# Pairing the two directions of a recurrence window by window, and loading the next phase's first strips early

## The reference

```
def _rwkv7_step(state, inp):
    r, w, k, v, kk, a = inp
    sa = jnp.einsum("dbhvk,dbhk->dbhv", state, kk)
    state = (state * w[..., None, :] - sa[..., None] * (kk * a)[..., None, :]
             + v[..., None] * k[..., None, :])
    return state, jnp.einsum("dbhvk,dbhk->dbhv", state, r)
```

## Time and profile before

| | |
|---|---|
| median of 3 runs | 6579.88 us (6574.34 to 6580.43) |
| the profiled execution | 6581.77 us, span 6579.9 us |
| PE busy | 5670.6 us, 86% of the span |
| DVE, ACT, POOL busy | 2987.5, 2063.0, 1877.6 us |
| mean granted TensorE clock | 0.935 of full speed |
| a tile of the recurrence (x2 of window 0 to the next tile's) | 1089.66 to 1242.65 us |
| the two recurrences | about 740 to 2053 us, and 5151 to 6463 us of the span |

### The profile page before, as it was taken

The page is one execution under the profiler, slowest core; times in us unless marked ns, Lnnn a source line. Parts: engine busy times, 40 slices in busy tenths (PEclk is TensorE's granted clock), DMA queues, the critical chain, the costliest instruction groups (busy, mean ns, idle before and its releaser), DMA issues. The chain is left out here.

```text
span 6579.9 us, 214205 instructions
## 1 busy us (share of the span) xinstructions
PE 5670.6 (86%) x92720; PEld 3807.5 (58%) x92720; DVE 2987.5 (45%) x6387; ACT 2063.0 (31%) x3451; POOL 1877.6 (29%) x2006
## 2 busy tenths in 40 slices
PE   5999788888887899977888895698999888888887
PEld 4555577777774455444554454544454677777773
DVE  7100366666663233145534367522300466666661
ACT  3000255454541312133422132311100354544440
POOL 4452144444441336000002631000000344444440
PEclk8999899999998999988899997899999899999998
DMA  3222100001112222122212237522112001110002
GB/s 130 100 90 84 45 31 31 31 31 43 36 37 76 106 100 79 44 84 68 60 48 91 95 96 96 127 72 85 65 65 74 35 31 39 37 39 31 31 31 93
DMA packets 192660, 425.81 MB, mean 65 GB/s; under 512 B 24384, under 2 KB 108224, under 8 KB 192192
## 3 DMA queue, kind: packets, MB, share of 16 engines
q1 hardware_dynamic: 157440, 322.85, 16.5%
q10 hardware_dynamic: 34752, 96.51, 3.7%
HBM read 313.41 MB, written 105.87 MB: 64 GB/s over the span
## 5 line engine op out<-in xcount | busy, mean ns | idle before, releaser
L382 PE MATMUL ps<-arena 128*128 128x512 f32 x4544 | 1686.0, 533 | 60.4 <-ACT arena L336 18.4
L382 PEld LDWEIGHTS ps<-arena 128*128 128x128 f32 x4544 | 862.9, 190 | 878.7 <-issue 810.5
L1890 PE MATMUL ps<-arena 64*64 64x64 f32 x35840 | 737.1, 226 | 172.1 <-issue 75.9
L158 POOL TENSOR_TENSOR arena<-arena 128x512 f32<-128x512 f32 (+1 forms) x360 | 338.9, 957 | 1700.3 <-DMA arena<-w_mod 1690.1
L1890 PEld LDWEIGHTS ps<-arena 64*64 64x64 f32 x35840 | 644.3, 138 | 244.7 <-issue 229.9
L2297 ACT COPY arena<-ps 128x512 f32<-128x512 f32 (+1 forms) x880 | 535.8, 626 | 411.7 <-PE ps L1890 403.1
L2442 POOL TENSOR_TENSOR arena<-arena 128x256 f32<-128x256 f32 (+1 forms) x320 | 316.6, 997 | 812.5 <-DVE arena L2683 533.7
L540 PE MATMUL ps<-arena 128*128 128x512 f32 (+1 forms) x1152 | 422.9, 527 | 18.2 <-ACT arena L336 18.2
L2367 POOL MEMSET arena<- 128x1280 f32 (+4 forms) x22 | 15.1, 739 | 1331.2 <-POOLq L88 1331.2
L161 POOL TENSOR_TENSOR arena<-arena 128x256 f32<-128x256 f32 (+2 forms) x504 | 376.5, 759 | 51.2 <-issue 0.2
L1698 ACT COPY arena<-ps 128x1280 f32<-128x1280 f32 (+1 forms) x64 | 75.0, 1172 | 963.5 <-PE ps L382 749.0
(11 more groups left out here) (269 smaller groups left out, 9762.3 us busy)
## 6 DMA issues: line engine op xcount, KB each, us to landing
arena<-proj SPq DMA_DIRECT2D x158, 640.0 KB, 5.1
proj<-arena ACTq DMA_DIRECT2D x80, 640.0 KB, 3.8
arena<-w_mod SPq DMA_DIRECT2D x96, 512.0 KB, 7.4
arena<-rw_w SPq DMA_DIRECT2D x68, 512.0 KB, 3.4
xres<-arena ACTq DMA_DIRECT2D x24, 640.0 KB, 6.1
arena<-na_w_in SPq DMA_DIRECT2D x24, 512.0 KB, 3.6
arena<-x SPq DMA_DIRECT2D x16, 640.0 KB, 6.7
arena<-xres SPq DMA_DIRECT2D x16, 640.0 KB, 6.0
```

The lines of the kernel that those rows point to most:

```text
L158: self.nc.gpsimd.tensor_tensor(out, strip[:, c:c + n, :], self.k.cond[:, c:c + n, s:s + 1].to_broadcast([P, n, P]), ALU.mult)
L382: last = nc.tensor.matmul(k.ps[:, 3 * u + n, 0:b - a], w[:, c * P:(c + 1) * P], src[:, c, a:b], start=(c == 0), stop=(c == KT - 1))
L1890: last = PE.matmul(part_of(out, dst, hh, g, d), part(l, src, hh, g, d), rhs, start=True, stop=True)
```

## The change

Window n now treats forward chunk group n together with backward group BACK[n] = (0, 4, 3, 2, 1)[n], so that the states of both directions can be carried inside the windows: each trip of PE's loop carries the four steps of the window before it. The separate 20 steps disappear. Maps of one window are kept in place of five. With it:

- BH against KK and BH against R are one set of 16 matmuls of 128 columns (the joined score set), in place of two sets of 64 columns.
- v differs between directions, so v has four transposes in place of two, and `local_outputs` 48 matmuls in place of 40.
- ACT takes over DVE's negated half behind `gh_mm` and the negated copy `zt`; DVE gets the steps and `state_outputs`; POOL gets `second_outputs` (where two directions meet in y) and, inside windows 0 to 3, `gate_values`, `keep_par`, `bonus_half` and `bonus_terms`.
- What is left between windows is the next tile's preparation and one normalisation. It now stands ahead of a tile's windows, also for the first tile; after the last tile the last four steps and two normalisations follow, one after the other.
- SP loads the output projection's first two strips and residual tiles (`early_loads`) once the last tile's operands are used; `dense_residual` waits for `k.early` in their place.

```diff
-STEPS_BACK = [c for s in ((0, NCTX // C), (NCTX // C, NCH)) for c in reversed(range(*s))]
-LOOP_FILL = (0, 24)
+BACK = (0, 4, 3, 2, 1)
+LOOP_FILL = (70, 69)
...
+            def step(n):
+                for d in range(2):
+                    at, col = map_of(d, n) * C, chunk_of(d, n) * C
+                    for hp in HP:
+                        PE.matmul(state_reads(d)[hp, col:col + C], Sst[hp, n % 2, d, :], QT[hp, at:at + C], start=True, stop=True)
+                    for hp in HP:
+                        last = PE.matmul(state_sums(d)[hp, :], TT[hp, at:at + C], Sst[hp, n % 2, d, :], start=True, stop=True)
+                    last.then_inc(s_mm[d], 1)
...
                 product(low[0], Yb, F, 2).then_inc(f2_mm, 1)
-                scores(low[1], BH_, R_).then_inc(m4_mm, 1)
+                pe.wait_ge(yw_ev, it + 1)
+                pe.wait_ge(q_ev, it + 1)
+                step(0)
                 pe.wait_ge(f2_ev, it + 1)
                 product(low[0], F, None, 3).then_inc(di_mm, 1)
+                states_seen(it, 1)
+                step(1)
...
+                states_seen(it, 3)
+                step(3)
                 pe.wait_ge(yzt_ready, it + 1)
                 pe.wait_ge(kb_ev, it + 1)
                 product(low[2], Ya, F, 5).then_inc(f3_mm, 1)
+                pe.wait_ge(y_ev, it + 2)
+                pe.wait_ge(v_kept, it + 1)
+                for d in range(2):
+                    for g in range(2):
+                        PE.transpose(bank[7][...], v_win[:, d, g * P:(g + 1) * P], k.ident)
+                        last = PE.transpose(bank[6][...], ops[:, KK_, d, g * P:(g + 1) * P], k.ident)
+                last.then_inc(kv_mm, 1)
...
+                    step(late, it, 0)
+                    step(late, it, 1)
+                    if n == 0:
+                        weighted(e)
+                    if n == 1:
+                        finished(e)
                     if n + 2 < NW2:
                         sums_scan(e, n + 2)
+                    step(late, it, 2)
                     if more:
                         operands_beta(e, n + 1)
+                    if n:
+                        step(late, it, 3)
+                    else:
+                        restart(it)
+                    state_outputs(late)
...
+                    for half in range(2):
+                        last = SC.mul(flat(RH[:, 4 * half:4 * half + 4, :]), bank[4 + half], -1.0)
+                    last.then_inc(gh_ev, 1)
...
+            for dst_, src_ in early:
+                sp.dma_start(dst_, src_).then_inc(k.early, 16)
```

More of the change, by code:

```diff
@@ L429, in _ @@
                 u = c % 2
+                if c < 2 and early:
+                    continue
                 if c >= 2:
@@ L1826, in tile_loads, with post_loads @@
                 sp.dma_start(par, dram_tile(k.A["rw_par"], e + (KT * j + off))).then_inc(tile_in, 16)
[L1828 to L1832, removed]
+            def post_loads(e, off):
+                sp.wait_ge(bonus_mm, e * 3 + 3)
+                for n, dst_ in ((0, r2), (1, k2)):
+                    sp.dma_start(dst_, dram_tile(k.proj, e + (n * KT + off))).then_inc(post_rk_in, 16)
@@ L1914, in gains @@
                                          RH[cp, hh * 4 + q, C:2 * C], start=False, stop=True)
[L1915 to L1919, removed]
+                last.then_inc(tt_mm, 1)
             def local_outputs():
[L1922 to L1928 removed]
@@ L1938, in turned_scores, with window @@
             def turned_scores():
-                scores(low[1], BH_, KK_).then_inc(xt_mm, 1)
-            def window(it, late, scored):
+                for d in range(2):
+                    for g in range(2):
+                        for hh in range(2):
+                            for c in range(2):
+                                at, col = (2 * g + c) * C, (g * 2 + d) * C
+                                last = PE.matmul(halves(pair[1][HP[c], hh, :])[:, :, col:col + C], ops[HP[hh], BH_, d, at:at + C],
+                                                 ops[HP[hh], KK_:R_ + 1, d, at:at + C], start=True, stop=True)
+                last.then_inc(xt_mm, 1)
+            def window(it, scored):
                 pe.wait_ge(xt_ev, it + 1)
@@ L2373, in betas @@
-            def betas(e, n, first=False):
+            def betas(e, n):
                 if n == 0:
@@ L2424, in keep_par, with second_outputs @@
                 pool.drain()
-            widen_kk(0)
-            betas(0, 0, True)
-            keys(0, 0)
-            keep_v(0, 0, True)
+            def second_outputs(unit, it):
+                pool.wait_ge(y_ev, it + 1)
+                hold(k, pool)
+                for d in range(2):
+                    if not first_touch(d, unit):
+                        at = y[:, cols((unit, BACK[unit])[d])]
+                        GP_.tensor_tensor(at, at, yt[:, d, :], ALU.add)
+                pool.drain().then_inc(y_sum, 1)
             for e in range(KT):
@@ new lines, in _ @@
+                sums_scan(e, 0)
+                sums_rest(e, 0)
+                for c in range(3):
+                    centred(e, MEAN_BANK, c)
+                for c in range(3):
+                    kk_unit(e, c)
+                bonus(e, BONUS_BANK, 0)
+                operands_beta(e, 0)
+                operands_kk(e, 0)
+                variance(e, VAR_BANK)
+                operands_r(e, 0)
+                bonus(e, BONUS_BANK, 1)
+                bonus(e, BONUS_BANK, 2)
+                post_inverse(e)
@@ L2793, in _ @@
-                mask_rest()
-                operands_keys(e + 1, 0)
-                sums(e + 1, 1)
+            it = KT * NW2 + 1
+            carried(NW2 - 1, it)
+            for c in range(3):
+                centred(KT, MEAN_BEFORE, c)
+            queries(it)
+            for n in range(4):
+                step(NW2 - 1, it, n)
+            state_outputs(NW2 - 1)
+            for c in range(3):
+                bonus(KT, BONUS_BEFORE, c)
+            variance(KT, VAR_BEFORE)
+            post_inverse(KT)
@@ L2797, in _ @@
+            for c in range(3):
+                scaled(KT, SCALE_BEFORE, c)
+            dve.drain()
+            weighted(KT)
             finished(KT)
             for c in range(3):
-                centred(KT, MEAN_LAST, c)
+                centred(KT + 1, MEAN_LAST, c)
             for c in range(3):
-                bonus(KT, BONUS_LAST, c)
-            variance(KT)
-            post_inverse(KT)
+                bonus(KT + 1, BONUS_LAST, c)
+            variance(KT + 1, VAR_LAST)
+            post_inverse(KT + 1)
```

923 lines of the change are left out of this document (422 added, 501 removed).

## The result

The changed kernel takes **7320.1 us** (median of 4 runs, 7302.7 to 7328.6) against 6577.1 before it on the same chip (4 runs, 6572.9 to 6580.4): ratio 1.113, interval 1.110 to 1.115. It is 743 us slower, where 29 us faster than this 6577.1 was forecast.

A forecast was written before the change was run, and what follows sets the result against it. PE was taken to bound the windows. Per layer: head +9.0, windows +141.6, inner stretches -128.8, end -37.7, together -15.9; twice -32 us, giving 6548 us. Range 6440 to 6650.

The forecast's parts named there:

- by the first the loop still fits: PE's window loop: with an instruction memory of 2048 instructions, the loop would stay in it after the change.
- Rival 4: PE's loop does not stay in instruction memory; window 0's stalls in each window, up to 2.7 x 64 = +173, 6720; chance 0.03.
- Windows: Windows 1 to 4 of a tile, walked through queue and waits: 95.6 us together against 77.2, 18.4 more.
- Rival 3: In windows, POOL's SBUF reads stretch DVE's `operands_kk` and state additions: +48 to +96, 6597 to 6645 us; chance 0.18.
- the wait before the transposes: In a window, PE waits 0.9 us before the v and kk transposes, which stand behind y_ev.
- The stretch: Between windows: 29.5 us of PE queue, 18.4 less than now, including 1.0 for PE's loop jumping back to overwritten code.
- Window 0: A tile's first window: 27.7 us, 0.7 less than now, including 0.9 of gaps where PE waits for nothing recorded.
- The head: Each layer's start, from data to window 0's x2, 24.8 us now: 9 us more.
- The end: Each layer's end, to the first strip's matmul: 52.5 us in place of 90.2, so -37.7.
- The early loads: At each layer's end, POOL's bonus product to the first strip's matmul falls from 26.0 by 3.5 to 22.5 us.
- rival 1: What the stretch gives, the windows take: plain windows 23.3 to 24.5 us, total 6548; chance 0.44.
- Rival 2: Waits in windows overlap more than walked: windows of 22.5 us, 64 x -1.4 = -90, total 6460; chance 0.31.

The follow-up runs named there:

- the aligned version: The changed kernel with filler counts LOOP_FILL 77 and 39 in place of 70 and 69, so PE's loops start at a block's start: 6669.0 us, ratio 1.0130.
- experiment 5: The aligned version with POOL's three long products taken out of windows 0, 2 and 3, to the stretch and window 4: 6620.8 us, ratio 1.0052.
- an exchange on the waiting engine: The aligned version with w's 32 matmuls ahead of the first scores on PE: 6689.1 us; together with experiment 5's edit and one-column fillers: 6571.9 us.

## Why the prediction was wrong

**The step that failed is the sentence "by the first the loop still fits".** Rival 4 named the mechanism, gave it 0.03, and priced it at 2.7 x 64 = 173 us. Three things in it were wrong. It compared the loop's length with 2048 instructions; the runs show a limit of 7 blocks of 256, counted from where the loop begins in its block, and the earlier trace rows show only that the loop of before fits, not with how much room. By my count there was one instruction of room. It left out `LOOP_FILL`, in the diff a change from (0, 24) to (70, 69), matmuls whose results nobody uses, which do little but move that place; I costed it at nothing and didn't ask what it was for. And it took one gap for a window's price, where a window fetches nine blocks and loses clock besides: 656 us between the aligned and the unaligned span, 10 us for each of 64 windows.

The Trainium skill, Runtime: NRT & Kernel Launch, section Instruction fetch mechanics, gives blocks of 256 instructions, and this case's gaps agree. It gives 2048 instructions for PE; here loops that end at 1884 and 2019 are fetched anew in every window, and one that ends at 1791 in none.

**The rest, read from the aligned version**, is a forecast of -32 us against a measured +90.2 (spans 6670.1 and 6579.9). Its 6669.0 us too lie above the predicted range of 6440 to 6650:

- Windows. Predicted 24.3, 23.9, 23.9 and 23.5, sum 95.6; measured 24.3, 25.5, 25.3, 23.0, sum 98.1. That is +40 us over 16 tiles. Rival 3 is the cause: with POOL's products moved they are 23.9, 23.8, 23.9, 23.05, sum 94.6, so the walk through the window was right to 1 us in 96. In part that is luck: in window 2 of experiment 5 the wait before the transposes is 0.22 us (predicted 0.9) and step 1 waits for nothing (0.3), while the first scores wait 1.40 (1.1). I priced the contention at 0.75 to 1.5 us in 64 windows; it was some 1.5 in 32 of them and 0.35 in 16, and through `operands_r` and f5, not through `operands_kk`. The Trainium skill, SBUF — State Buffer, section Who interferes with whom, says that a DVE instruction with two SBUF inputs contends with a GpSimd instruction that reads SBUF, and experiment 5 agrees: 3.27 us beside POOL, 0.69 without. The wait before the first scores was 1.40 to 1.78 (predicted 1.1).
- The stretch. Token sums to x2 took 27.4 us in the second stretch (predicted 28.5), but 3.0 pass before it, where PE fetches (I took 1.0).
- Window 0. Predicted 27.7, of which 0.9 for gaps; measured 32.1 in the second stretch's window, with fetch gaps of 1.57, 1.94, 0.71 and 1.47 and a stretch at the lower clock. The code between windows displaces the loop, and its first trip fetches it again. I had laid the gaps to the V2 and G2 loads, and moved them away with these. Stretch and window 0 together are 61.3 and 62.4 in place of 57.2: +65 us over 14.
- The head. In the first recurrence `gh` of the first window comes 16.6 us later than before, in place of 8.3: fillers hold PE from 752.7 to 769.3. In the second it is 9.2 later, counted from the start of the first output projection. Together +9.
- The end. From the last `gh` to the first strip 91.8 us before, 58.0 aligned: -33.8, predicted -37.7. In the other layer 92.6 and 57.0: -35.6. The early loads gave their 3.5. Together +6.

40 + 65 + 9 + 6 = 120 of the 122 between -32 and +90. Near balance (rival 1) was right for the windows' dependencies (23.8 in place of 23.9, with POOL's products moved) and useless as a forecast, since fetches decided. Rival 2 was nowhere near.

## What to carry to other kernels

A loop's length is not the question on PE; the question is how many blocks of 256 instructions it touches from where it begins. Count them when a loop grows, when code ahead of it changes, and whenever a diff contains unexplained fillers; check the queue that fetches instructions for packets inside the loop, and look for gaps "issue" in the middle of a product. Then compare kernels only with the loop aligned in both, or a difference of 651 us that belongs to the placement will be put down to the design. Operations of POOL that read SBUF for 3 us are best where DVE has no two-input work on the path; and an exchange on the waiting engine should be tried again after the other wait is gone (+15 to +20 us alone, a gain behind the other edit).

## What was unexpected of the hardware

- Two fillers more made a kernel 200 us slower; seven more and thirty fewer made another 651 us faster.
- A loop that enters its eighth block by 7 to 63 instructions is fetched about every second trip (9 blocks, then none); by 92 or more, every trip (9 blocks).
- The fillers, 64x64 matmuls that all use the same quarter of PE and one bank of PSUM, take 0.216 us each, and as long with 1 column as with 64 (16.58 and 16.68 us for 77). Going round the four quarters and two banks, 13 took 1.11 us in place of 3.04, both at a granted clock of 0.50. Which of the two it was that helped isn't shown.
- POOL's product takes 3.52 us whether DVE's is beside it or not; DVE's pays all, 0.69 to 3.27.
